# Start addresses in SBUF: weight remainders and moving operands at other offsets from a 128-byte line

## The reference

```
mod = silu(c) @ w_ada + b_ada                       # 2048 x 12288
h = rmsnorm(x, g0) * (1 + sc_m) + sh_m
q, k, v, g_ret, u, gate_r, gate_s = split(h @ w_in)
y_ret = (silu(g_ret) * group_norm(retention(rope(q), rope(k), v))) @ w_ret_out
a, b = split(gelu(s5_ssm(u)) @ w_s5_glu);  y_s5 = a * sigmoid(b)
y = (sigmoid(gate_r) * y_ret + sigmoid(gate_s) * y_s5) @ w_out
x = x + gt_m * rmsnorm(y, g1)
a, b = split(h2 @ w_ffn_in);  y = (silu(a) * b) @ w_ffn_out      # 5632 wide
x = x + gt_f * rmsnorm(y, g3)
# block 2: attention, gated linear attention and short convolution beside each other,
# their outputs merged by sigmoid gates, @ w_out_2; then a second FFN of 5632 and a last norm
```

## The kernel before

| tensor | bytes past a line |
|---|---|
| ring_raw, ring_lo, ring_hi, all four slots | 0 |
| h_split, ffn1_split, ffn2_split (shown as ffn_split), o_att, o_gla, y_conv | 32 |
| merged_split, y_ssm_split, ret_split, v_heads, u | 64 |
| mixed_split, att_q, att_k | 0 |
| s5_b, s5_c, s5_x | 96 |
| aside_d | 32 |
| aside_y, aside_z, aside_u | 64 |
| aside_s, aside_r | 96 |
| wa_lo and wa_hi (square k is 64 k further) | 32 |

## Time and profile before

### The profile page before, as it was taken

One profiled execution on the slowest core, in us unless ns is written; L12 is line 12 of the kernel. 1 busy time (PEld: TensorE's weight loads), 2 busy tenths in 40 slices (PEclk: granted clock), 3 DMA queues, 4 the chain that ended last, 5 costly groups with the idle time before them and its releaser, 6 DMA issues.

```text
span 3379.9 us, 51972 instructions
## 1 busy us (share of the span) xinstructions
PE 3307.3 (98%) x20368; PEld 2937.2 (87%) x20368; DVE 2324.5 (69%) x2503; ACT 1452.4 (43%) x1464; POOL 435.2 (13%) x309
## 2 busy tenths in 40 slices
PE   6999999999899999999899999999999999999998
PEld 3599999999788888888788888888888888888887
DVE  6789979877766666666666667566767766666554
ACT  2256664444443444433454443444344444344332
POOL 1047668500100000000000000000003000000000
PEclk9999999999999999999999999999999999999999
DMA  9885456678545555577534444555555555555554
GB/s 378 349 328 180 180 202 237 251 292 311 198 175 188 192 191 186 195 268 254 198 137 169 167 162 178 193 183 186 192 186 196 188 188 186 189 192 186 185 191 149
DMA packets 119746, 706.34 MB, mean 209 GB/s; under 512 B 13776, under 2 KB 28752, under 8 KB 41312
## 3 DMA queue, kind: packets, MB, share of 16 engines
q1 hardware_dynamic: 109280, 695.96, 56.2%
q10 hardware_dynamic: 10368, 9.02, 0.8%
HBM read 702.83 MB, written 2.10 MB: 209 GB/s over the span
## 4 chain that ended last, share of the span: by engine, by line
PE 90%; DVE 5%; ACT 1%; DMA 1%; SPq 1%; issue 1%; DVEq 0%; ACTq 0%
PE acc L638 45%; PE acc L639 24%; PE acc L635 6%; PE acc L636 6%; PE acc L637 6%; DVE ring_raw L1499 1%; DVE ring_lo L1477 1%; DMA ring_raw<-w_ada 1%; SPq L542 1%; PE p_y L705 1%; PE p_norm L687 1%; PE p_z L715 1%; ACT ring_hi L1017 0%; DMA ring_raw<-w_out 0%; DVE rstd L1524 0%
## 5 line engine op out<-in xcount | busy, mean ns | idle before, releaser
L638 PE MATMUL acc<-h_split,ring_hi 128*128 128x512 f32 x4736 | 1655.9, 392 | 9.5 <-DVE h_split L1539 4.5
L1477 DVE TENSOR_TENSOR ring_lo<-ring_raw,ring_hi 128x2048 fp32r<-128x2048 f32 (+2 forms) x560 | 1265.1, 2260 | 550.2 <-ACT ring_hi L1017 549.1
L639 PE MATMUL acc<-h_split,ring_lo 128*128 128x256 f32 x4736 | 1337.6, 282 | 0.0
L1017 ACT ACTIVATE ring_hi<-ring_raw 128x2048 fp32r<-128x2048 f32 (+2 forms) x560 | 1040.0, 1862 | 458.6 <-DMA ring_raw<-w_down 150.4
L638 PEld LDWEIGHTS acc<-h_split,ring_hi 128*128 128x128 f32 x4736 | 891.9, 188 | 197.6 <-issue 10.0
L639 PEld LDWEIGHTS acc<-h_split,ring_lo 128*128 128x128 f32 x4736 | 897.9, 190 | 0.4
L638 PE MATMUL acc<-ffn_split,ring_hi 128*128 128x512 f32 x1408 | 488.2, 390 | 0.0
L2146 POOL TENSOR_TENSOR sq_sum<-sq_sum,tile 128x256 f32<-128x256 f32 x60 | 79.6, 1326 | 2561.6 <-ACT tile L1043 2561.6
L639 PE MATMUL acc<-ffn_split,ring_lo 128*128 128x256 f32 x1408 | 397.1, 282 | 0.0
L635 PE MATMUL acc<-h_split,ring_hi 128*128 128x256 f32 x1152 | 329.2, 286 | 0.3 <-ACT val_a L1030 0.2
L637 PE MATMUL acc<-h_split,ring_lo 128*128 128x256 f32 x1152 | 321.6, 279 | 0.0
(11 more groups left out here) (381 smaller groups left out, 3936.5 us busy)
## 6 DMA issues: line engine op xcount, KB each, us to landing
ring_raw<-w_ff SPq DMA_DIRECT2D x88, 1024.0 KB, 4.8
ring_raw<-w_down SPq DMA_DIRECT2D x64, 1024.0 KB, 4.8
ring_raw<-w_ffb SPq DMA_DIRECT2D x56, 1024.0 KB, 4.8
ring_raw<-w_mix SPq DMA_DIRECT2D x48, 1024.0 KB, 4.8
ring_raw<-w_ada SPq DMA_DIRECT2D x32, 1024.0 KB, 11.9
ring_raw<-w_heads SPq DMA_DIRECT2D x32, 1024.0 KB, 4.8
ring_raw<-w_ret SPq DMA_DIRECT2D x32, 1024.0 KB, 5.2
ring_raw<-w_glu SPq DMA_DIRECT2D x32, 1024.0 KB, 4.9
```

The costliest lines, as they stand in the source:

```text
L638: mm(dst[:], hi[s][:, t, :], moving[:, k, :], start=start, stop=False, skip_group_check=True)
L639: return mm(dst[:, T:], lo[s][:, t, :], moving[:, k, 0:T], start=False, stop=stop, skip_group_check=True)
L1017: run(hi[s][:, 0:n, :], raw[s][:, 0:n, :], COPY).then_inc(hi_done, 1)
L1477: tt(lo[s][:, 0:n, :], raw[s][:, 0:n, :], hi[s][:, 0:n, :], SUB).then_inc(lo_done, 1)
```

## The change

It adds tensors that nothing uses, and by them moves the start addresses of others. No instruction is changed. In the ring, gaps of 0, 32, 64 and 96 bytes stand before ring_raw/ring_lo of slots 0 to 3, and the rest of 128 bytes after them, so that ring_hi of each slot is on a line again. The gaps add 512 bytes in all, so what follows the ring keeps its place modulo 128, except behind a further gap: 32 bytes before v_heads and before ret_split, 64 bytes after merged_split, 32 before ffn1_split and 64 before ffn2_split. Modulo 128 that gives ring_lo 0, 32, 64, 96 in slots 0 to 3; h_split, o_att, o_gla and y_conv 32 as before, merged_split 64 and mixed_split 0 as before; ret_split and v_heads 96 instead of 64, ffn1_split 64 and ffn2_split 96 instead of 32, y_ssm_split and u 0 instead of 64, and s5_b, s5_c, s5_x 32 instead of 96.

```diff
@@ -212,9 +212,12 @@
         raw, hi, lo = [], [], []
         for s in range(SLOTS):
+            if s:
+                sb(ctx, f"ring_gap{s}", [P, 8 * s])
             with ExitStack() as shared:
                 raw.append(sb(shared, f"ring_raw{s}", [P, KT, P]))
             lo.append(sb(ctx, f"ring_lo{s}", [P, KT, P], F32R))
+            sb(ctx, f"ring_step{s}", [P, 32 - 8 * s])
             hi.append(sb(ctx, f"ring_hi{s}", [P, KT, P], F32R))
@@ -251,12 +254,15 @@
                 with ExitStack() as shared:
+                    sb(shared, "v_step", [P, 8])
                     v_heads = sb(shared, "v_heads", [P, HEADS, 4, T])
                 with ExitStack() as shared:
+                    sb(shared, "ret_step", [P, 8])
                     ret = sb(shared, "ret_split", [P, HEADS, 2, 2 * T], F32R)
...
                 merged = sb(mixer, "merged_split", [P, KT, 2 * T], F32R)
+                sb(mixer, "y_step", [P, 16])
@@ -310,6 +316,7 @@
             with ExitStack() as ffn:
+                sb(ffn, "f1_step", [P, 8])
                 f1 = sb(ffn, "ffn1_split", [P, FF, 2 * T], F32R)
@@ -380,6 +387,7 @@
             with ExitStack() as ffn:
+                sb(ffn, "f2_step", [P, 16])
                 f2 = sb(ffn, "ffn2_split", [P, FF, 2 * T], F32R)
```

## The result

The changed kernel takes 3411.51 us (median of 3, 3411.38 to 3413.67) against 3381.87 before: a ratio of 1.008 with a 95% interval of 1.0066 to 1.0094, slower by 30 us. The forecast was 3386, with a range up to 3405. The profiled execution took 3413.67 us, with a span of 3411.9, which is 32.0 over that of before. Of all executions behind this document one stands out, one of e4's ten with 4991.44 us against 3380.41 to 3388.98 for the other nine; its ratio leaves it out.

What follows compares the result with a forecast made beforehand. TensorE, busy 98% of the span, was taken to bound the kernel, so time is steps times step length. Terms by stage, from -1.1 (f1) to +3.4 us (y_ssm), summed to +4.7 on 3381.6, giving 3386; range 3358 to 3405.

Steps and rivals of the forecast that it cites:

- Counting steps by slot: Ring matmuls: number of steps times change in step length, such as 4736 h pairs, 1184 a slot.
- The modulus: Ring matmuls: each load step priced by distance between moving operand and loaded weights modulo 128, today the moving offset.
- Each half by itself, averaged: h pairs against shifted remainders: prices by slot give +0.8 us, a second reading +3.2; +2.0 taken.
- Distance 64 for pairs: f1 pairs: high halves' loads get distance 64, priced -1.5 ns each over 704 pairs, -1.1 us.
- Rival A: Distance 64 also good for pairs, 13.7 ns less in h's slot 3 and f1: 3360 us, chance 0.26.
- Branch outputs and h thirds: Three branch outputs' 384 pairs priced as h, +0.1 us; 1152 h thirds at 0.2, +0.2 us.
- y_ssm +3.4: y_ssm thirds, moved from 64 to 0: 13.3 ns x 256 = +3.4 us; mean duration rising from 277 to about 281.
- mixed -0.5: mixed pairs, staying on the line: remainders go from +2.2 to +0.2 ns over 256 pairs, -0.5 us.
- the work off the path: DMAs and VectorE on shifted raw tiles and remainders: 1.8 us of cover, so nothing shows; counted 0.
- Rival B: Off-line weights keep the rhythm from settling in slots 1 to 3, +3.3 ns x 4896 pairs: 3405 us, chance 0.20.
- Rival C: Remainder's address counts for nothing; only y_ssm, f1, f2 and ret move: 3383 us, strictly 3381.6; chance 0.12.
- wa's last eleven steps: wa_hi and wa_lo, only off-line weights in the earlier trace: 350.0 ns against 346.7, bounding a shifted pair at +3.3 ns.

Runs made afterwards that it cites:

- e4: Every address, weights and moving operands alike, moved 32 bytes together against the kernel before, all distances kept: 3384.8 us, 1.0003.
- e13: Only the ring's gaps, word for word as in the diff, added to the kernel before; moving operands not moved: 3414.93 us, 1.0083.
- e1: Only the ring's gaps, equal to the diff's modulo 128 but not modulo 256, added to the kernel before: 3398.72 us, 1.0047.
- e5: Whole ring, remainders and high halves, moved 128 bytes against its moving operands, f1 64 and f2 96 bytes further, against the kernel before: 3392.46 us, 1.0022.
- e6: Against the kernel before, all slots with h 224 bytes from ring_lo and 160 from ring_hi, modulo 256, (224, 160); other moving operands shifted: 3401.61 us, 1.0059.
- e12: The changed kernel's four placements with slots 1 and 2 exchanged, moving gaps as in the diff: 3396.87 us, 1.0039 against the kernel before.
- e2: Only the moving operands' gaps (f1, f2, ret, y_ssm) added to the kernel before, all weights on the line: 3394.72 us, 1.003.
- e11: All four slots placed as slot 3 of the changed kernel, h at (64, 32), its moving gaps kept: 3425.04 us, single execution.
- e10: All four slots placed as slot 1 of the changed kernel, h at (128, 32), its moving gaps kept: 3402.5 us, single execution.
- e9: Against the kernel before, all slots alike with h, FFN, branch-output and mixed pairs at (0, 64) from remainder and high half: 3347.53 us, 0.9904.
- e7: Against the kernel before, high halves 128 bytes further on than remainders in all slots, h at (32, 160), other moving operands shifted: 3404.11 us, single execution.
- e8: Against the kernel before, high halves 192 bytes on in all slots; h at (32, 96), f1 (64, 128), f2 (0, 64): 3386.58 us, single execution.

## Why the prediction was wrong

Counting steps by slot was right: the table's sum gives the change of the span within 2 us, and nothing else moved. The prices were wrong. The ring's gaps alone lengthen the steps (e13, +34.3 us in the span), since a step follows both distances modulo 256 and the products around it. The step that failed is "I count by the distance d between the moving operand and the weights that are being loaded, modulo 128: today it is the moving offset for both halves."

1. *The modulus.* 128 is too small; 256 fits all runs. e1 and e13 are equal modulo 128 and 16 us apart; e5 moves the ring by 128 and takes mixed from 351.0 to 353.3. The three offsets of the earlier trace rows were too few to tell 128 from 256, and mixed, taken as 0, was at 128. So "ring_hi of each slot is on a line again" did not mean that it stayed: its distance from h goes 160, 32, 160, 32. The prediction counted the high halves of h as untouched.
2. *Each half by itself, averaged.* "1184 x (0 + 2.2 + 0 - 1.5) ns = +0.8 us", taken as +2.0, measured +18.9. What a pair takes is not a sum of one price for each half: (0, 64) takes 340.0, (64, 64) and (0, 0) both 353.3, which would add up to 366.6 for (64, 0); mixed in e6 has (64, 0), and takes 350.0. And it depends on the products around it, by e12 and by e13 beside e1. The slots were forecast at 346.7, 349, the same and 345; only slot 0 came so.
3. *Distance 64 for pairs.* Price -1.5 for f1's high halves; e2 has (64, 64) at 353.3, +6.6 a pair. Merged's fast thirds do not carry over to pairs. Rival A is thus wrong for both of its places (slot 3 at 352.1, f1 at 348.9), although the size of gain it looked for exists, at (0, 64).
4. *Branch outputs and h thirds*, +0.1 and +0.2, measured +2.0 and +4.0, for the same reason as in 2.
5. *Near in number, by luck:* y_ssm +3.4 (measured +3.1; its mean duration went from 277 to 281 as said) and mixed -0.5 (-0.4). Both come from prices that fail in points 1 and 2. Mixed's slots were to take 351, 349, 347 and 349 and take 347.6, 352.2, 346.5 and 351.8; only their mean is met. y_ssm was priced at 0 from mixed, which was at 128, and its high halves are at 0 and 128 by turns. merged has the sign (+0.9, measured +2.4); ret was to be -0.5 and is +0.7.
6. *Right:* the work off the path cost nothing, and TensorE has no idle time before L647. The fp32 steps did not change, but they were no test, since their distances did not change either.
7. *Rival B* had the nearest time, 3405, but not the mechanism: by e4 weights off the line cost nothing while the distances stay. *Rival C* falls with e13, and its claim that the remainder's address counts for nothing with e13 beside e1 and e11 beside e10. The Trainium skill ("SBUF — State Buffer", Who interferes with whom) has TensorE wait on nobody. The trace agrees that nothing waits, but not, as rival C took it, that the address is therefore free: the pair runs at 340.0 (e9) or 351.2 ns (changed kernel) with no idle time in either window.

The range ended at B's own time, since a shifted pair's price was bounded by wa's last eleven steps. The bound that was needed is the worst steady pair, 353.3 against 346.7, on all pairs: the thirds at 353 in the earlier trace rows gave its size, since three thirds and a pair stream the same 768 columns.

One rule of reading from ahead of the prediction also needs care. Durations were to be comparable within one kind of matmul, but h's pairs at a step of 346.7 show 390 ns before, 391 in e5 and 393 in e7's first FFN, and e6's at 343.3 show 389. A change of a few ns in a duration does not give the change of the step.

## What to carry to other kernels

Where TensorE is busy without idle time and its steps are longer than their columns, read the step by buffer slot, start to start; one median of durations hides that slots differ. Start addresses are worth an experiment: among the kernels timed with an interval, unused gaps alone made from +1.0% to -1.0%. What is to be tried is the distances of the moving operand from the weights that it meets. With equal distances in all slots there are few combinations, and the best kernel here (e9) has them equal; but unequal ones are not dearer as such (e12 against the changed kernel). Look at several executions, since those of e9, at the same addresses, lie some 20 us apart. A gap that is zero modulo a supposed line length is not a gap of nothing until a run says so.

## What the runs showed of the hardware

- The fp32r pair (512 and 256 columns, each with its own 128-column weight load) settles mostly at steps of 340.0, 343.3, 346.7, 350.0 or 353.3 ns when all slots are alike, with some placements between (351.1 at (128, 128), 352.0 at (0, 128), 348.9 at (128, 32)). The lowest, 340.0, is 20 ns over the 320 of its 768 columns at 2.4 GHz; no placement tried went below.
- Steps at seen distances, for pairs: (0, 64) 340.0; (32, 32), (160, 160), (32, 96), (64, 128), (192, 128) 346.7; (96, 96), (128, 192) about 350; (64, 64), (0, 0), (224, 224), (0, 192), (64, 192), and (64, 32) in the FFNs, 353.3. Moving all addresses by 32 changes no pair; y_ssm's thirds went from 344.2 to 351.8, between their two rhythms of 340 and 353.
- Distances alone do not fix the step. In one kernel, (224, 160) gives 343.3 for h in the FFNs and 352 in mrg0 and for the branch outputs (e6), (32, 160) gives 346.6 in the first FFN and 350.0 in the second (e7), and thirds at (64, 64) run at 340.0 (merged) or 352.7 (ret) in the kernel before. From kernel to kernel, (0, 192) gives f1 353.3 in all slots of e6 and 341.2 in slot 1 of e12. What selects the rhythm was not found.
- Plain fp32 matmuls kept their durations, 378 to 379 and 380 ns. No kernel changed the distance between their operands, so whether it matters is not shown.
- Open: what in the chip makes the dependence, since the trace shows lengths and no cause; whether e12 is cheaper because the high half's distance changes twice a round or because the remainders come in another order; and the spread between executions at (0, 64) and in e6. One execution of each was profiled, near the low end of its spread, so what is longer in the others was not seen. The steps of e7, e8, e10 and e11 come from the only execution of each.
